# Changing where the fp32r operands of four stages start in SBUF: padded rows and staggered phases

## What is computed

```
for l in range(DEPTH):                                  # DEPTH = 2
    x = x + 0.5 * swiglu_ffn(rms_norm(x, g1[l]), ffn1_w_in[l], ffn1_w_out[l])
    proj = rms_norm(x, g2[l]) @ w_mix_in[l]
    x = x + concatenate([y_rwkv, y_moba]) @ w_mix_out[l]
    x = x + memory_cross_attention(...)                 # w_q, w_kv, w_o
    x = x + 0.5 * swiglu_ffn(rms_norm(x, g4[l]), ffn2_w_in[l], ffn2_w_out[l])
...
x = x + gate1 * (merged @ w_out)                        # second block
for e in range(N_EXPERTS):
    act = silu(hf @ w_gate[e]) * (hf @ w_up[e])
    y = y + combine[:, e:e + 1] * (act @ w_down[e])
x = x + gate2 * y
```

## Time and profile before

| | |
|---|---|
| three runs | 1977.76 us median, 1976.09 to 1980.92 |
| profiled execution, from its first to its last instruction | 1974.9 us, granted clock 0.994 |
| PE / PEld / DVE / ACT / POOL busy | 97 / 85 / 70 / 55 / 4% of the span |
| instructions | 34,249, of them 14,092 matmuls |
| DMA | 404.03 MB, mean 205 GB/s; in the expert stage (1700 to 1900 us) 375 GB/s |

### The profile page before, as it was taken

The page is one execution under the profiler, slowest core; times in us unless marked ns, Lnnn a source line. Parts: engine busy times, 40 slices in busy tenths (PEclk is TensorE's granted clock), DMA queues, the critical chain, the costliest instruction groups (busy, mean ns, idle before and its releaser), DMA issues. The chain is left out here.

```text
span 1974.9 us, 34249 instructions
## 1 busy us (share of the span) xinstructions
PE 1920.4 (97%) x14092; PEld 1679.4 (85%) x14092; DVE 1377.6 (70%) x1960; ACT 1092.7 (55%) x1645; POOL 81.6 (4%) x93
## 2 busy tenths in 40 slices
PE   7999998999999999999989999998999999999999
PEld 5888987999888888889879988887998998888888
DVE  5675875675666666666756665656776769999997
ACT  5444672554544544457545554444555457777775
POOL 1000006000000000000140000000000000000000
PEclk9999999999999999999999999998999999999999
DMA  9765330443665556544215455653333339999995
GB/s 386 282 234 184 137 127 24 148 163 139 245 249 204 205 207 254 213 153 161 72 47 193 150 217 213 245 188 136 126 119 119 130 113 352 356 372 377 373 371 198
DMA packets 56646, 404.03 MB, mean 205 GB/s; under 512 B 6376, under 2 KB 6560, under 8 KB 8240
## 3 DMA queue, kind: packets, MB, share of 16 engines
q1 hardware_dynamic: 51504, 370.73, 50.7%
q0 software_dynamic: 4992, 31.15, 4.1%
HBM read 400.80 MB, written 1.06 MB: 203 GB/s over the span
## 5 line engine op out<-in xcount | busy, mean ns | idle before, releaser
L306 DVE TENSOR_TENSOR weights_split<-ring,weights_split 128x1024 fp32r<-128x1024 f32 x696 | 819.6, 1221 | 206.3 <-ACT weights_split L296 202.4
L296 ACT CAST weights_split<-ring 128x1024 fp32r<-128x1024 f32 x696 | 693.4, 1048 | 214.2 <-PE ps L329 200.7
L327 PE MATMUL ps<-weights_split,act 128*128 128x512 f32 (+1 forms) x896 | 334.4, 373 | 12.7 <-DVE weights_split L306 12.6
L329 PE MATMUL ps<-weights_split,act 128*128 128x512 f32 (+1 forms) x896 | 329.3, 367 | 0.0
L328 PE MATMUL ps<-weights_split,act 128*128 128x512 f32 (+1 forms) x896 | 328.8, 367 | 0.0
L327 PEld LDWEIGHTS ps<-weights_split,act 128*128 128x128 f32 x896 | 168.9, 189 | 40.8 <-DVE weights_split L306 12.6
L329 PEld LDWEIGHTS ps<-weights_split,act 128*128 128x128 f32 x896 | 168.8, 188 | 28.6
L328 PEld LDWEIGHTS ps<-weights_split,act 128*128 128x128 f32 x896 | 169.1, 189 | 26.3
L327 PE MATMUL ps<-act,weights_split 128*128 128x256 f32 x608 | 175.3, 288 | 0.3
L329 PE MATMUL ps<-act,weights_split 128*128 128x256 f32 x608 | 170.5, 280 | 0.0
L328 PE MATMUL ps<-act,weights_split 128*128 128x256 f32 x608 | 170.4, 280 | 0.0
(11 more groups left out here) (549 smaller groups left out, 3370.8 us busy)
## 6 DMA issues: line engine op xcount, KB each, us to landing
ring<-stream SPq DMA_DIRECT2D x348, 1024.0 KB, 4.9
stretch<-ada_in POOLq DMA_DIRECT2D x24, 1024.0 KB, 5.1
y<-c_in POOLq DMA_DIRECT2D x4, 512.0 KB, 6.2
act_room<-mem_in SPq DMA_DIRECT2D x2, 1024.0 KB, 4.8
consts<-w_consts SPq DMA_DIRECT2D x1, 1376.0 KB, 11.7
x<-x_in SPq DMA_DIRECT2D x1, 1024.0 KB, 4.9
stretch<-mem_in POOLq DMA_DIRECT2D x1, 1024.0 KB, 9.6
bias_t<-bias_scratch POOLq DMA_DIRECT2D x1, 1024.0 KB, 12.0
```

The costliest lines, as they stand in the source:

```text
L296: core.nc.scalar.copy(self.hi[:, self.place(i), part], core.slot(chunk)[:, part]).then_inc(self.rounded.sem, 1)
L306: core.nc.vector.tensor_tensor(self.lo[:, self.place(i), part], core.slot(chunk)[:, part], self.hi[:, self.place(i), part].bitcast(F32), A ...
L327: nc.tensor.matmul(out, lhs[0], rhs[0], start=start, stop=False, **kw)
L329: return nc.tensor.matmul(out, lhs[1], rhs[0], start=False, stop=stop, **kw)
```

## The change

A new function `staggered` lays a tile out with a pitch wider than its row, at a phase of its own. Nothing is computed differently and no engine gets another instruction or another order of them; the one difference in the instructions themselves is that accesses which ran through two or more blocks without a gap have one dimension more (`mlp_hidden_lo`, 128x512 before, 128x2x256 after).

```diff
+    def staggered(self, name, shape, dt, ctx, phase, pitch):
+
+        return self.phased(name, [*shape[:-1], pitch], dt, ctx, phase)[..., 0:shape[-1]]
+
...
-        hid_hi = core.phased("mlp_hidden_hi", [P, 2, 2, S], F32R, ctx, EVEN)
-        hid_lo = core.phased("mlp_hidden_lo", [P, 2, 2, S], F32R, ctx, EVEN)
+        hid_hi = core.staggered("mlp_hidden_hi", [P, 2, 2, S], F32R, ctx, 0, S + 16)
+        hid_lo = core.staggered("mlp_hidden_lo", [P, 2, 2, S], F32R, ctx, 256, S + 16)
...
-        a_hi = core.phased("slot_hi", [P, TILES, KB, SLOTS], F32R, ctx, EVEN)
-        a_lo = core.phased("slot_lo", [P, TILES, KB, SLOTS], F32R, ctx, EVEN)
+        a_hi = core.staggered("slot_hi", [P, TILES, KB, SLOTS], F32R, ctx, 0, SLOTS + 1)
+        a_lo = core.staggered("slot_lo", [P, TILES, KB, SLOTS], F32R, ctx, 160, SLOTS + 1)
...
-        hid_hi = core.phased("hidden_hi", [P, 2, 2, SLOTS], F32R, ctx, EVEN)
-        hid_lo = core.phased("hidden_lo", [P, 2, 2, SLOTS], F32R, ctx, EVEN)
+        hid_hi = core.staggered("hidden_hi", [P, 2, 2, SLOTS], F32R, ctx, 320, SLOTS + 8)
+        hid_lo = core.staggered("hidden_lo", [P, 2, 2, SLOTS], F32R, ctx, 336, SLOTS + 8)
...
+        def sums_blocks(tile, half):
+            return sums_bank(tile, half).rearrange("p (k s) -> p k s", s=SLOTS)
+
         def sums_slot(part, tile, half):
-            return part[:, tile, :, :].rearrange("p k s -> p (k s)")[:, half * 512:(half + 1) * 512]
+            return part[:, tile, 4 * half:4 * half + 4, :]
...
-                    nc.scalar.copy(sums_slot(a_hi, tile, half), sums_bank(tile, half)).then_inc(sums_rounded.sem, 1)
+                    nc.scalar.copy(sums_slot(a_hi, tile, half), sums_blocks(tile, half)).then_inc(sums_rounded.sem, 1)
...
-        hi, lo = (core.phased(name, [P, KB, S], F32R, ctx, ODD) for name in ("y_hi", "y_lo"))
+        hi, lo = (core.staggered(name, [P, KB, S], F32R, ctx, phase, S + 1) for name, phase in (("y_hi", 32), ("y_lo", 64)))
...
-        hi, lo = (core.phased(name, [P, KB, S], F32R, ctx, ODD) for name in ("act_hi", "act_lo"))
+        hi, lo = (core.staggered(name, [P, KB, S], F32R, ctx, phase, S + 1) for name, phase in (("act_hi", 96), ("act_lo", 128)))
```

More of the change, by code:

```diff
@@ L2141, in subtract_sums @@
                     dve.wait_ge(sums_rounded.sem, sums_rounded.at(2 * tile + half + 1))
-                    nc.vector.tensor_tensor(sums_slot(a_lo, tile, half), sums_bank(tile, half),
+                    nc.vector.tensor_tensor(sums_slot(a_lo, tile, half), sums_blocks(tile, half),
                                             sums_slot(a_hi, tile, half).bitcast(F32),
```

## The result

The changed kernel is slower: 1992.95 us median (1990.52 to 1994.99, 4 runs) against 1977.95 us (1976.09 to 1980.92, 4 runs), a ratio of 1.0068 with a 95% interval of 1.005 to 1.0087. I had forecast 1963.9 us with a range of 1944 to 1988, so the time lies outside the range and on the other side of no change. The medians are 15.0 us apart; the ratio on record, which is not the quotient of the medians, makes it 13.5 us (9.9 to 17.2). The profiled execution took 1994.99 us, its span 1993.2.

What follows compares the result with a forecast made beforehand. PE, busy 97% of the span, was taken as the bound through the summed start-to-start distances of its matmuls. Five gains, 2.8 + 0.6 + 5.5 + 0.8 + 4.2 = 13.9 us, gave 1963.9 us, with a range of 1944 to 1988.

Steps and rivals of the forecast that it cites:

- the bounds: Per fp32r matmul: at best 10.4, 10.0, 8.7 or 7.1 ns saved by placement; loss not excluded, nearest size 2.9 ns.
- part by part: Whole change: counts of matmuls times a gain of 2.9 ns each, five terms summing to 13.9 us.
- terms 1 and 5: Stationary `mlp_hidden` (inner values), 960 matmuls, 2.8 us gained; experts, 1,440 matmuls, 4.2 us gained.
- term 3: Moving `y`, 768 matmuls, 2.2 us gained, and second stage's moving `act_hi/lo`, 1,152 matmuls, 3.3 us gained.
- `mlp_hidden` moving: Second term: 192 matmuls with `mlp_hidden` as moving operand, 0.6 us gained, best 1.9.
- `act_hi/lo` stationary with `to_tokens`: Fourth term: 192 matmuls with stationary `act_hi/lo` and 80 of `to_tokens`, 0.8 us gained.
- The writers: VectorE writing the tiles: a second block costs 0 to 157 ns, 40 times, covered by other work; zero taken.
- Odd words: Rival: `slot`, `y`, `act` starting at any word lose 2.9 ns in 3,152 matmuls, 9.1 us, 1986.9; slower overall 0.22.
- Full relief: Rival: new phases keep the two operand reads apart altogether, 35 us gained, 1943 us; chance 0.12 (gain over 25 us).
- The bound by DMA: Experts: weights cap the gain at 0.20 us a unit, some 7 us; as rival 1968 us, within the forecast's 0.38.

Runs made afterwards that it cites:

- experiment 4: Changed layout's gaps and extra dimensions on `mlp_hidden`, `hidden`, `slot_hi`, relative phases kept modulo 256 bytes, `y` untouched, against the kernel before: ratio 0.9999 (0.9986 to 1.0012).
- experiment 5: Kernel before with every fp32r tile, weights too, 32 bytes further, so relative phases stay the same: ratio 0.9994 (0.9982 to 1.0006).
- experiment 1: Kernel before with only `mlp_hidden` staggered, in steps of 64 bytes, lo from 256: ratio 1.0023 (1.0014 to 1.0033), 4.6 us slower.
- experiment 2: Kernel before with only the expert stage's `slot` and `hidden` staggered: ratio 1.0036 (1.0024 to 1.0048), 7.1 us slower.
- experiment 3: Kernel before with only `y` and the second stage's `act_hi/lo`, moving operands, staggered: ratio 1.0007 (0.9996 to 1.0017), 1.4 us.

## Why the prediction was wrong

**What bounds the kernel** was right: PE's time is the sum of distances, a longer distance was paid in full, and the loss is accounted for by counts times differences and the experts' stretch (14.8 of 15.0 us). It was right too that placement changes the distance of fp32r matmuls. The Trainium skill's rule, from "TensorE: Matmul & The Clock Gate", "Part 2: What happens when you issue a matmul", that the load of the next weights takes nothing from the running matmul, would have given no change; experiments 4 and 5 against 1 and 2 show that equal work at other relative places costs about 5 ns more a matmul (226.7 and 231.4), so for fp32r the runs decide against what follows from it, that placement does not matter. One reading of mine was loose: the eight records of the earlier trace rows are four matmuls of two passes each, so it is a pass of 256 columns, not the float32 matmul, that takes as long as 512 columns of fp32r. The 2.9 ns are then those of a pass with its own load, and the bounds stay.

**The step that failed** is the second half of the part by part: "I take a gain of one step, 2.9 ns, because [...] one common phase for all blocks has been replaced by many, which makes the worst meeting rarer." I took the placement of before at 512 columns for a bad one, since its overhead of 13.3 ns is large beside 2.9 ns of float32. None of the other placements that the runs have there is cheaper: no mean came under 226.7 ns. So terms 1 and 5 had the wrong sign, and term 3 too, where 116.7 ns became 118.1 (`y`) and 119.2 (`act_hi/lo`). The row that misled me was the difference between the earlier trace rows, both at 256 columns with weights stationary; there 32 is better than 0. At 512 columns with weights moving 32 is 6.4 ns worse than 0. The sign does not carry over from one shape and role to another, and I had no row at 512 columns but one. The ends of my bounds said as much (nothing excluded a loss), but the size at that end, the same 2.9 ns, was about half of what six of the eight other uniform phases cost in the products of 24, 5.2 to 6.9 ns.

By terms, forecast and measured: inner values stationary -2.8 and +4.6 us; `mlp_hidden` moving -0.6 and about 0; `y` and `act_hi/lo` -5.5 and, by distances, +4.0, by the ratio of experiment 3 +1.4 (-0.8 to 3.4); `act_hi/lo` stationary with `to_tokens` -0.8 and about +0.3 (119.1 ns for 118.3, 118.2 for 116.9); experts -4.2 and +7.1 by the ratio of experiment 2, +6.3 in the changed kernel's profile. The writers, which I had at nothing, are at nothing where it was measured: 692 ns for 691, and experiment 4 at 0.9999 with the gaps of three tiles.

**The rivals.** Odd words had the sign and two thirds of the size (9.1 us forecast, 13.5 by the ratio) and not the cause of most of it: `mlp_hidden` and `hidden` have no odd words and lost about half of the sum (4.5 us, and 480 matmuls of some 6 ns), and a stationary operand at 12 costs less than one at 32. My sign for it, 119 ns or more for `y` and `act`, did appear in `act_hi/lo`; for moving operands the rival stays open in part. The placement at 144, no odd word, costs 118.6 ns and the odd words 76 and 12 cost 117.5 and 117.4, so it is no rule there either. That steps of 32 or 64 bytes could cost was no case of mine, which is why the range ended at 1988. Full relief is out. The line of 16 bytes that the Trainium skill gives for SBUF ("SBUF — State Buffer", "Door 1: The DMA port swizzle") bears on this less than I allowed: a stationary block at phase 32 begins with a whole line and one at 12 does not, and they cost 233.1 and 226.7 ns in the products of 24, 233.3 and 230.0 in the last 36 matmuls. The bound by DMA that I set over the experts never came to bear, since there was no gain to stop; going the other way nothing was hidden, the unit of the earlier trace rows paid 0.17 us for 36 matmuls.

**Open.** What in SBUF or in the load of operands repeats after 256 bytes, why the cost of one operand shows at its neighbours, and what decides into which rhythm a stretch settles, the runs do not tell. The meeting of the two reads is argued, not shown: what is shown is the dependence on the relative place and on how the stretch begins.

## What to carry to other kernels

Before moving operands by some bytes, read which placements the trace already has for the same shape and the same roles, and take no sign from another shape; with one placement in the trace, the sign is open and the present one may be the best. A large overhead per matmul is by itself no sign of a bad placement. A profile with one phase per stage maps several placements in one run, where the total time needs ten runs for 2 us; but read each placement in more than one stretch, since equal placements differed by 1 ns between executions and by up to 6.7 ns within one.

## What the runs showed of the hardware

- fp32r matmuls with a 128-column stationary load: the distance depends on where the two operands start relative to each other (0 and 256 equal, 32 and 288 equal; all tiles 32 further equal). At 512 moving columns the mean of a placement is 226.7 ns at best and up to 233.6; at 256 columns 113.3 to 123.2.
- It depends on what came before too. At 512 columns 0 and 256 settle to 226.7 ns in every down product; 12, 16 and hi/lo at 0/40 or 40/256 have it in the products of 24, which follow a gate_up at 226.7, and 230.0 to 233.3 in the last 36 matmuls, which follow transposes. At 256 columns a stationary operand at 76 ran at 113.3 and at 120.0 ns in two blocks of the same stage.
- Most stretches that an experiment does not touch agree to 0.02 us between profiles (22.48 or 22.49 us for the earlier trace rows in before, after and experiments 1 to 4). Not all do: the 192 matmuls with `act` moving at 32 that stand just before that stretch's counterpart in layer 1 take 22.66 us in before and 22.86 in experiment 1, which left them alone, 1 ns each, in another rhythm and at full clock.
- The clock falls to 1.2 GHz at other places in other executions. Before, it did so for 3.4 us at 949.1, at the start of the second stage (1351.8), after a stretch in which PE was busy 11.18 of 13.80 us, and for 3.4 us each at 1433.8 and 1624.9; in experiment 2 the fall at 1433.8 is absent and one of 13.7 us stands at 1602.6. From the last matmul of `mlp_hidden` to the first of `slot_hi`, equal code, the first takes 268.4 us and the second 271.4, 3 us that are near the size of what experiment 3 had to show. The view by windows of before (columns as in the earlier trace rows), then of experiment 2:

```profile
1351.80:1365.50 13.70, 10.64 (x46) 9.91 (x46) 11.05 (x28) 8.15 (x14) 0.00 (x0) 0.50 0.27 99
1338.00:1351.80 13.80, 11.18 (x93) 10.63 (x92) 5.88 (x23) 4.23 (x9) 0.54 (x1) 1.00 0.04 8
1433.80:1437.20 3.40, 3.40 (x19) 3.40 (x18) 3.29 (x6) 0.88 (x1) 0.00 (x0) 0.50 0.18 24
```

```profile
1434.00:1437.00 3.00, 3.00 (x26) 2.95 (x26) 2.96 (x5) 1.40 (x2) 0.00 (x0) 1.00 0.02 5
1602.60:1616.30 13.70, 13.29 (x64) 13.02 (x64) 7.96 (x33) 4.17 (x7) 0.00 (x0) 0.50 0.38 154
```
